# Stick-breaking attention of a decoder step: running sums over high and low parts, a new order of the pairs, absolute values shared between two engines

## The reference, cut to what matters

```python
z = jnp.einsum('bqhd,bkhd->bhqk', qb, kb).astype(jnp.float32) * scale + bias
log_1m = jnp.where(mask, jax.nn.log_sigmoid(-z), 0.0)
log_w = jax.nn.log_sigmoid(z) + lax.cumsum(log_1m, axis=3, reverse=True) - log_1m
w = jnp.where(mask, jnp.exp(log_w), 0.0)
outs.append(jnp.einsum('bhqk,bkhd->bqhd', w.astype(vb.dtype), vb))
```

## Time and profile before

| what | us |
|---|---|
| median of 3 runs (lowest, highest) | 2427.94 (2426.88, 2428.55) |
| the profiled execution | 2428.46 |
| its span | 2426.8 |
| PE busy | 2382.4 |
| DVE busy | 1241.0 |
| ACT busy | 994.5 |
| granted clock over the span | 0.998 |

### The profile page before, as it was taken

The page is one execution under the profiler, slowest core; times in us unless marked ns, Lnnn a source line. Parts: engine busy times, 40 slices in busy tenths (PEclk is TensorE's granted clock), DMA queues, the critical chain, the costliest instruction groups (busy, mean ns, idle before and its releaser), DMA issues.

```text
span 2426.8 us, 43808 instructions
## 1 busy us (share of the span) xinstructions
PE 2382.4 (98%) x18802; PEld 2183.8 (90%) x18802; DVE 1241.0 (51%) x1725; ACT 994.5 (41%) x1399; POOL 114.9 (5%) x232
## 2 busy tenths in 40 slices
PE   6999999999999999999999999999999999999998
PEld 5999999965699999999999999887777999999998
DVE  5533246755576333357523347755554758633245
ACT  5422235635456222346422245533223546522243
POOL 0000000122100000000000000012222100000000
PEclk9999999999999999999999999999999999999999
DMA  8555345785537653565754255544545456642254
GB/s 308 180 183 183 124 149 179 252 211 139 190 113 228 215 173 95 188 206 175 261 184 156 83 168 189 188 153 165 170 165 165 136 177 182 206 126 88 87 179 155
DMA packets 122660, 417.10 MB, mean 172 GB/s; under 512 B 23387, under 2 KB 27611, under 8 KB 122211
## 3 DMA queue, kind: packets, MB, share of 16 engines
q1 hardware_dynamic: 88962, 301.92, 39.1%
q10 hardware_dynamic: 18144, 62.03, 7.1%
q0 software_dynamic: 15360, 50.34, 6.3%
HBM read 390.84 MB, written 23.41 MB: 171 GB/s over the span
## 4 chain that ended last, share of the span: by engine, by line
PE 88%; DVE 5%; ACT 3%; DMA 2%; issue 1%; SPq 0%; ACTq 0%; POOL 0%; DVEq 0%; POOLq 0%
PE PS L2026 70%; PE PS L1425 3%; PE PS L1960 2%; DVE WL L2318 2%; PE PS L1990 2%; PE PS L1355 1%; ACT WH L2140 1%; DMA AFIRST<-in_w_ada 1%; PE PS L791 1%; PE PS L1309 1%; PE PS L1340 1%; PE PS L1350 1%; PE PS L753 1%; DMA RAW<-in_w_out 1%; PE PS L1321 1%
## 5 line engine op out<-in xcount | busy, mean ns | idle before, releaser
L2318 DVE TENSOR_TENSOR WL<-RAW,WH 128x1024 fp32r<-128x1024 f32 (+1 forms) x478 | 633.0, 1325 | 647.9 <-ACT WH L2140 647.2
L2026 PE MATMUL PS<-HH,WH 128*128 128x260 f32 x3432 | 796.6, 285 | 3.2 <-DVE QKVS L1119 1.8
L2026 PE MATMUL PS<-HH,WL 128*128 128x260 f32 x3432 | 786.5, 283 | 0.0
L2026 PE MATMUL PS<-HL,WH 128*128 128x260 f32 x3368 | 769.6, 283 | 0.0
L2140 ACT ACTIVATE WH<-RAW 128x1024 fp32r<-128x1024 f32 (+1 forms) x478 | 542.2, 1135 | 425.4 <-PE PS L2026 267.0
L2026 PEld LDWEIGHTS PS<-HH,WH 128*128 128x128 f32 x3432 | 569.9, 188 | 25.4 <-issue 16.8
L2026 PEld LDWEIGHTS PS<-HH,WL 128*128 128x128 f32 x3432 | 569.4, 188 | 0.0
L2026 PEld LDWEIGHTS PS<-HL,WH 128*128 128x128 f32 x3368 | 557.0, 188 | 0.6 <-issue 0.2
L2026 PE MATMUL PS<-GH,WH 128*128 128x260 f32 x1408 | 386.4, 285 | 0.9 <-DVE WL L2318 0.8
L2026 PE MATMUL PS<-GL,WH 128*128 128x260 f32 x1408 | 384.2, 283 | 0.0
L2026 PE MATMUL PS<-GH,WL 128*128 128x260 f32 x1408 | 383.5, 283 | 0.0
(11 more groups left out here) (340 smaller groups left out, 2317.5 us busy)
## 6 DMA issues: line engine op xcount, KB each, us to landing
RAW<-in_w_in SPq DMA_DIRECT2D x236, 512.0 KB, 3.7
RAW<-in_w_out SPq DMA_DIRECT2D x120, 704.0 KB, 4.0
AW<-in_w_ada ACTq DMA_DIRECT2D x114, 512.0 KB, 5.5
RAW<-in_w_odd SPq DMA_DIRECT2D x60, 512.0 KB, 3.7
RAW<-in_w_odout SPq DMA_DIRECT2D x30, 512.0 KB, 3.9
RAW<-in_w_even SPq DMA_DIRECT2D x28, 512.0 KB, 4.0
KV<-in_v_pages POOLq DMA_DIRECT2D x32, 256.0 KB, 4.8
SR<-in_ret_past POOLq DMA_DIRECT2D x32, 256.0 KB, 4.0
```

The lines of the kernel that those rows point to most:

```text
L2026: last = nc.tensor.matmul(ps[:, x, 0:HT], w[:, k * P:(k + 1) * P], src[k0 + k][:, x, :], start=(begin and t == 0), stop=(end and t == 2))
L2318: nc.vector.tensor_tensor(low_, RAW[:, from_:from_ + w], high_.bitcast(F32), ALU.subtract).then_inc(lo_done, 1)
```

## The change

It touches the mixer of the first layer alone.

- `sums` multiplies in fp32r: ACT copies the softplus rounded to fp32r into one of two places SPH (`high_part`), DVE takes the difference into SPL (`low_part`), which lies on SP itself, and each group runs both parts against fp32r copies TRIR and ONESR of the triangle and the ones: 20 fp32r matmuls for a head, where there were 10 in fp32.
- `log_weights` writes into SP, and ZS is free after it; SP has five places (`HOME_OF`).
- `sized` (absolute value by DVE) is for heads 0 to 3, ACT takes it for heads 4 to 7 (`decay`).
- The last units of evin have side work at four places. The scores of head 1, `sums_past` and, on ACT and DVE, the work on head 0 up to its high and low part stand in units 25 to 27.
- After evin, PE interleaves the scores of pair 1 with the sums of head 0; in the loop a turn runs sums, `values_past`, sums, all scores of pair t + 2, and the values of pair t.
- The outputs of k and of the pooling rows are issued before the loads of evout instead of between them, under a semaphore `pool_out` of their own, and the pooling rows are written 16 wide (`US[:]`); the host drops the first.

```diff
+HOME_OF = (0, 1, 2, 3, 0, 4, 2, 3)
+SP = [SQ5[n] for n in HOME_OF]
+SPL = [SL5[n] for n in HOME_OF]
+SPH = [at("SHA", [CAUSAL], sph_at, F32R)[:], at("SHB", [CAUSAL], sph_at + causal, F32R)[:]]
+TRIR = at("TRIR", [P], acc_at, F32R)
+ONESR = at("ONESR", [P], acc_at + size([P]), F32R)
...
-        if i == 3:
+        if i == 0:
             sp.wait_ge(ev_act, EV_FULL)
             sp.wait_ge(ev_dve, EV_FULL)
             for dst, src in ((k_t[:, 0:4 * SEQ], KP[:]), (k_t[:, 4 * SEQ:4 * SEQ + 32], QKVS[:, 4:8, :]),
-                             (pool_p, UP[:, :, SEQ + 1:SEQ + 16]), (pool_n, US[:, :, :, 1:16])):
-                sp.dma_start(dst, src).then_inc(out_done, 16)
+                             (pool_p, UP[:, :, SEQ + 1:SEQ + 16]), (pool_n, US[:])):
+                sp.dma_start(dst, src).then_inc(pool_out, 16)
+        if i == 3:
...
+        h, j = divmod(n, 3)
-            pe.wait_ge(z_dve, n)
+            pe.wait_ge(z_dve, 4 * h + j)
+        if n == 3:
+            pe.wait_ge(pool_low, 5)
...
+    POOLED_AT = {(23, 4): 0, (24, 2): 1, (24, 4): 2, (25, 2): 3}
+    SCORES_AT = {(25, 3): 0, (25, 4): 1, (26, 1): 2, (26, 2): 3, (26, 3): 4, (26, 4): 5}
+    def side(i, quarter):
+        if quarter == 4 and i in (22, 23, 24, 25):
             scores_past(i - 22)
+        if (i, quarter) == (26, 2):
             turn_past()
+        if (i, quarter) in POOLED_AT:
+            pooled(POOLED_AT[i, quarter])
+        if (i, quarter) in SCORES_AT:
+            first_scores(SCORES_AT[i, quarter])
+        if (i, quarter) == (27, 3):
+            sums_past()
...
-    def scores_of_one():
-        for j in range(4):
-            pe.wait_ge(vp_evac, 2) if j < 2 else pe.wait_ge(z_dve, 3 + j)
-            score(1, j, PS[0][:, j % 2, 0:LEN[j]]).then_inc(z_done, 1)
+            side(i, 4)
     def scores(t, j):
-        if t == PAIRS:
+        if t >= PAIRS:
             return
-        pe.wait_ge(z_dve, biased_to(t, j))
+        if t == 1 and j == 0:
+            pe.wait_ge(vp_evac, 2)
+        else:
+            pe.wait_ge(z_dve, 8 * t + 2 * j)
         for e in range(2):
             score(2 * t + e, j, PS[0][:, e, 0:LEN[j]]).then_inc(z_done, 1)
     def sums(h, i):
         if i == 0:
-            pe.wait_ge(sp_done, h + 1)
+            pe.wait_ge(spl_done, h + 1)
+        if h + i == 0:
+            pe.wait_ge(const_ok, 3)
         n = 4 * h + i
         pe.wait_ge(lw_done, n - 1) if n >= 2 else pe.wait_ge(vp_evac, 4)
-        last = nc.tensor.matmul(PS[1][:, i % 2, 0:LEN[i]], TRI[:], SP[h % 4][:, OFF[i]:OFF[i] + LEN[i]],
-                                start=True, stop=(i == 3))
-        for j in range(i + 1, 4):
-            last = nc.tensor.matmul(PS[1][:, i % 2, (j - i) * P:LEN[i]], ONES[:],
-                                    SP[h % 4][:, OFF[j]:OFF[j] + LEN[j]], start=False, stop=(j == 3))
+        for j in range(i, 4):
+            w = TRIR if j == i else ONESR
+            for x, part in enumerate((SPH[h % 2], SPL[h])):
+                last = nc.tensor.matmul(PS[1][:, i % 2, (j - i) * P:LEN[i]], w[:],
+                                        part[:, OFF[j]:OFF[j] + LEN[j]], start=(j == i and x == 0),
+                                        stop=(j == 3 and x == 1))
         last.then_inc(s_done, 1)
...
-    sums_past()
-    scores_of_one()
+    for j in range(4):
+        scores(1, j)
+        sums(0, j)
     ada_step("start", 0)
     for t in range(PAIRS):
-        scores(t + 1, 0)
-        sums(2 * t, 0)
-        scores(t + 1, 1)
         if t:
-            values(t - 1)
-        sums(2 * t, 1)
-        scores(t + 1, 2)
-        sums(2 * t, 2)
-        if t == 2:
-            gather(0)
-        scores(t + 1, 3)
-        sums(2 * t, 3)
-        if t < 3:
-            values_past(t)
+            for i in range(4):
+                sums(2 * t, i)
+        values_past(t)
         ada_step("head", 2 * t)
         for i in range(4):
             sums(2 * t + 1, i)
+        if t == 1:
+            gather(0)
+        for j in range(4):
+            scores(t + 2, j)
+        ada_step("head", 2 * t + 1)
         if t == 3:
-            values_past(3)
-        ada_step("head", 2 * t + 1)
-    gather(1)
-    values(3)
+            gather(1)
+        values(t)
...
     def decay(h):
-        act.wait_ge(z_masked, 4 * h + 4)
-        nc.scalar.activation(SP[h % 4], ZS[h % 4], ACT.Abs).then_inc(z_act, 1)
-        act.wait_ge(z_act, h + 1)
-        nc.scalar.activation(SP[h % 4], SP[h % 4], ACT.Exp, scale=-1.0).then_inc(e_done, 1)
+        if h > 3:
+            act.wait_ge(z_masked, block_of(h, 3))
+            act.wait_ge(o_done, h // 2 - 1)
+            nc.scalar.activation(SP[h], ZS[h], ACT.Abs).then_inc(z_abs, 1)
+        act.wait_ge(z_abs, h + 1)
+        nc.scalar.activation(SP[h], SP[h], ACT.Exp, scale=-1.0).then_inc(e_done, 1)
     def log(h):
         act.wait_ge(e_done, h + 1)
-        nc.scalar.activation(SP[h % 4], SP[h % 4], ACT.Ln, bias=ONES[:, 0:1]).then_inc(l_done, 1)
+        nc.scalar.activation(SP[h], SP[h], ACT.Ln, bias=ONES[:, 0:1]).then_inc(l_done, 1)
+    def high_part(h):
+        act.wait_ge(sp_done, h + 1)
+        if h == 0:
+            act.wait_ge(pool_out, 64)
+        after(act, s_done, 4 * (h - 2) + 4)
+        nc.scalar.activation(SPH[h % 2], SP[h], ACT.Copy).then_inc(sph_done, 1)
     def weights(h):
         act.wait_ge(lw_done, 4 * h + 4)
-        nc.scalar.activation(SP[h % 4], ZS[h % 4], ACT.Exp).then_inc(w_done, 1)
+        nc.scalar.activation(SP[h], SP[h], ACT.Exp).then_inc(w_done, 1)
...
     for t in range(PAIRS):
+        if t == 0:
+            weights(0)
+        if t < 3:
+            decay(2 * t + 2)
+            decay(2 * t + 3)
+            table(LOG_SET)
+            log(2 * t + 2)
+            log(2 * t + 3)
+            table(EXP_SET)
         if t:
             outputs(t - 1)
+            weights(2 * t)
+        weights(2 * t + 1)
         if t < 3:
-            decay_of_pair(t + 1)
-            table(LOG_SET)
-        if t < 3:
-            for h in (2 * t + 2, 2 * t + 3):
-                log(h)
-            table(EXP_SET)
-        for h in (2 * t, 2 * t + 1):
-            weights(h)
+            high_part(2 * t + 2)
+            high_part(2 * t + 3)
...
+    def sized(h):
+        dve.wait_ge(z_dve, block_of(h, 3))
+        dve.wait_ge(z_masked, block_of(h, 3))
+        nc.vector.scalar_tensor_tensor(SP[h], ZS[h], -1.0, ZS[h], ALU.mult, ALU.max).then_inc(z_abs, 1)
     def softplus(h):
+        if h >= HEADS:
+            return
         dve.wait_ge(l_done, h + 1)
-        dve.wait_ge(z_dve, 4 * h + 4 if h < 2 else sized_to(h // 2, h % 2))
-        nc.vector.scalar_tensor_tensor(SP[h % 4], ZS[h % 4], 0.0, SP[h % 4], ALU.max,
-                                       ALU.add).then_inc(sp_done, 1)
+        nc.vector.scalar_tensor_tensor(SP[h], ZS[h], 0.0, SP[h], ALU.max, ALU.add).then_inc(sp_done, 1)
+    def low_part(h):
+        dve.wait_ge(sph_done, h + 1)
+        nc.vector.tensor_tensor(SPL[h], SP[h], SPH[h % 2].bitcast(F32), ALU.subtract).then_inc(spl_done, 1)
     def log_weights(h, i):
         dve.wait_ge(s_done, 4 * h + i + 1)
-        z = ZS[h % 4][:, OFF[i]:OFF[i] + LEN[i]]
-        nc.vector.tensor_tensor(z, z, PS[1][:, i % 2, 0:LEN[i]], ALU.subtract).then_inc(lw_done, 1)
     def scored(t, j):
-        if t == PAIRS:
+        if t >= PAIRS:
             return
         if j == 0:
-            after(dve, w_done, 2 * t - 2)
-            if t == 1:
-                dve.wait_ge(out_done, 96)
+            after(dve, lw_done, 8 * (t - 1))
         for e in range(2):
             dve.wait_ge(z_done, 8 * t + 2 * j + e + 1)
             biased(2 * t + e, j, PS[0][:, e, 0:LEN[j]])
...
+            first_scored(0, 0)
+            first_scored(0, 1)
+            first_scored(0, 2)
+            first_scored(0, 3)
+            pooled_samples()
+            sized(0)
+            dve.wait_ge(pool_out, 64)
+            first_scored(1, 0)
+            first_scored(1, 1)
+            ada_evac("evin", i)
+        if i == 27:
+            first_scored(1, 2)
+            first_scored(1, 3)
+            ada_evac("evin", i)
+            sized(1)
+            low_part(0)
...
     dve.wait_ge(zn_pe, 2)
+    nc.vector.tensor_tensor(ZN[:, 0, :], ZN[:, 0, :], PS[2][:, 0, :], ALU.subtract).then_inc(zn_dve, 1)
     dve.wait_ge(unit_done, POS["evin"] + len(EV))
-    nc.vector.tensor_tensor(ZN[:, 0, :], ZN[:, 0, :], PS[2][:, 0, :], ALU.subtract).then_inc(zn_dve, 1)
-    scored_one()
+    scored(1, 0)
     nc.vector.tensor_copy(VSR[0:NS, :], PS[3][0:NS, 1, :]).then_inc(vs_ok, 1)
     dve.wait_ge(vs_ok, 1)
-    nc.vector.memset(PS[3][:, 1, :], 0.0).then_inc(pz_ok, 1)
+    nc.vector.memset(PS[3][:, 1, :], 0.0).then_inc(z_zero, 1)
+    log_weights(0, 0)
+    scored(1, 1)
+    log_weights(0, 1)
+    softplus(1)
+    scored(1, 2)
+    log_weights(0, 2)
+    scored(1, 3)
+    log_weights(0, 3)
+    sized(2)
+    low_part(1)
+    sized(3)
     for t in range(PAIRS):
-        if t == 2:
+        if t:
```

(35 more changed lines are left out.)

169 lines of the change are left out of this document (78 added, 91 removed).

## The result

The median after the change is 2440.97 us (2439.22 to 2443.39, five runs), before it 2428.55 (2426.88 to 2432.22): a ratio of 1.0049 with an interval of [1.0034, 1.0063], 0.5% slower. The prediction was 2431.3, in a range up to 2437. The change is slower, as forecast, but by 12.4 us and not by 3.4, so the prediction was wrong on size. The execution in the profile took 2440.05 us, with a span of 2438.4.

The account below looks back on a forecast made before the run. PE, busy for 98% of the span, was taken as the bound. Stretch terms 0.4 + 7.9 - 1.9 - 3.4 gave +3.0 us, raised to +3.4 for missed small delays: 2431.3 us, range 2426.5 to 2437.

Parts of the forecast that it names:

- The sums: On PE, a head's sums would take 3.1 us instead of 4.79, sparing 1.7 a head, 13.6 for eight heads.
- my lower bound: In the sums, an fp32r product of 128 columns takes at least 0.06 us; 0.10 was assumed.
- The scores in a row: Four score blocks in sequence between PE and DVE: steps of 2.6, 2.1, 1.6 and 0.43 us, 6.8 in all.
- The chain behind: After the last scores, DVE's biased scores, softplus and low part take 5.1 us; PE waits another 1.8 before the next sums.
- The earlier output of k costs nothing: it goes while PE is in evin, whose loads are far ahead: During evin, issuing k's output earlier was claimed to add 0 us.
- no more than 3 us: Bound on the early k output: without cover it would delay a gather by its own transfer, at most this.
- The clock: Rival: thin PE work between scores and sums drops the clock, 6.3 us more each of two times, 2444 us; chance 0.04.
- PE is there after 13.3 and waits 1.1: At the last values_past, pages land after 14.4 us; PE arrives after 13.3 and waits 1.1.
- The new order as such: In the attention, the reordered work and split sums together were laid out as +3.0 us, raised to +3.4.
- the four stretches: PE from scores_past(1) to first values_past, sums of head 2, sums of head 6, first output product: 62.7, 20.2, 40.7, 18.2 us.
- The layout: Step-by-step schedule of PE's work and waits through the attention, giving +3.0 us; 2428 to 2435 by itself, weight 0.66.
- the three named: PE's waits before the change: 1.05 us for the samples' softplus, 0.99 for head 1's, 0.34 at pair 3.

Follow-up runs that it names:

- e3: The change with unread filler matmuls in the waits between the blocks of scores of pairs 2 and 3: 2443.87 us, ratio 1.0059.
- e2: The kernel before with only k's two outputs issued early, ahead of evout's first load: 2439.07 us, ratio 1.0040.
- e1: The change with k's two outputs back at their old place, the pooling rows still early: 2437.52 us, ratio 1.0034.
- e7: e1 with the sums in fp32 again, without high and low parts, in the new order: 2441.43 us, ratio 1.0047.
- b1_split: The kernel before in its own order, with split fp32r sums for all heads and pooling rows in whole lines: 2447.71 us, ratio 1.0073.
- b3_odd: The kernel before in its own order, with the sums of heads 3, 5 and 7 alone split: 2428.66 us, ratio 0.9996.

## Why the prediction was wrong, and where it was right

**The sums: right in total, by the luck of two misses that cancel.** 3.31 us a head; I had 3.1, and 3.4 with waits for PS[1]. The short products cost less than I took:

```profile
604.51 0.22 PE L811 MATMUL PS<-SHA,ONESR 128*128 128x128 f32 x1
604.57 0.27 PE L811 MATMUL PS<-SCL,ONESR 128*128 128x128 f32 x1
```

0.06 us, my lower bound. At the measured spacings the 20 products make 2.3 us, and 0.24 us for each of the four groups is left, where I had 0.1. FP8 and Floating Point Precision (TensorE Precision Notes), of the Trainium skill, led to an estimate of 2.4 us for a head; the products alone come to that, but no head does, the waits for PS[1] included in its time.

**The scores in a row: right. The chain behind: about right.** Steps of 2.69, 2.15 and 1.67 us for 2.6, 2.1 and 1.6. Waits for a low part of 1.0 us at heads 4 and 6, none at head 2, where I had 1.8 to 2.8; the lower clock had stretched the values ahead of them, and e3 brought the waits back, 1.81 and 2.85 at heads 2 and 4.

**"The earlier output of k costs nothing: it goes while PE is in evin, whose loads are far ahead": wrong**, the step that failed worst. I asked whether evin's weights had slack, and not whose loads share the time: `scores_past(2)` needs eight page loads of 256 KB, asked for from 510 us on, and k goes at 512.5. They took 7.6 us to land (median), not 3.6. PE waited 4.16 us and then ran 3 us longer at the lower clock. My bound, "no more than 3 us", had the transfer and left out what follows a wait. The pooling rows, moved to the same place, have their share: with only k early the wait is 0.84 us (e2), with only the pooling rows early 0.70 (e1). I had only asked what their whole lines free, and not what their new place costs. DMA: Bandwidth & Descriptors (Issuing engines are not separate DMA queues), of the Trainium skill, says that transfers of all issuing engines run on the same 16 DMA engines and interleave; the trace agrees: POOL's page loads and SP's output are on different queues, and the loads landed 1.7 to 4.0 us later with the outputs beside them.

**The clock, given a chance of 0.04: happened, at four places.** I named the place between scores and sums and its price, 6.3 us each time. The price was wrong: the modulation step and the values took 2.5 us longer (5.77 us from 597.58 to 603.35, for 1.0 + 2.3), and most of that replaced a wait: e3 got back 0.9 and 0.7 us. Ahead of the first `values_past` the lower clock took 3.0 in the change; in e1_k_late 0.9, at the modulation step at 575.3 us. TensorE: Matmul & The Clock Gate (HAM oscillation), of the Trainium skill, warned of such a relapse for groups of matmuls between waits. The trace agrees with it in kind; the 2444 that I gave for this rival was nearer to the 2441 than my forecast, but by luck: no stretch bears out its 6.3 us.

**"PE is there after 13.3 and waits 1.1": half right.** The wait for the last value pages was 2.31 us, and behind it `values_past` ran at a clock of 0.58, 4.02 us for its first ten products which took 2.32 in the call at 606.67. These 1.2 and 1.7 us are what is missing at the end, 2.7.

**The new order as such: mis-sized.** I had +3.0 us for order and split together. e1_k_late, the change without the early k, is +8.4, and e7, without the split as well, +11.3. In e1's profile the four stretches are 1.9, 1.7, 0.4 and 2.6 us longer than laid out. The layout had no term for the clock, which explains 0.9 us in the first stretch, 1.6 in the last (3.87 us for the first ten products of `values_past`, for 2.32) and, by e3, some 0.9 in the second. Waits for pages explain another 0.70 in the first and 1.1 in the last. The rest, 1.4 us, stays open. The prediction also read the old order as better than it is: the longest wait there for biased scores is not among the three named,

```profile
613.96 0.92 PE L685 MATMUL PS<-QP,KP 64*128 64x384 f32 x4 [1.49 <-DVE ZD L1056]
```

so the exchange of scores between PE and DVE cost something before too.

## What to carry to other kernels

A shorter product on the bounding engine is worth its time only where the passes that feed it have slack: list for each consumer when its input is ready and when it is wanted, and change only those with a gap. Before moving a large output, look at every load in flight in the stretch it moves to, on any queue, and price a late load as its wait plus, where the wait is long, the work behind it at half the clock (the waits of 0.70 and 0.84 us left the clock at 1.00, that of 4.16 did not). When a wait is filled or a clock restored, look for the next wait before counting the gain.

## What was not expected of the hardware

- Outputs of 1 MB (k) and 256 KB (pooling rows) beside page loads of 256 KB doubled their landing, 3.6 to 7.6 us; k alone made it 5.3 and the pooling rows alone 6.0. POOL's own issues went from 1.15 us apart to 2.1 (514.60, 516.71, 518.85).
- Writing 4096 pieces of 60 bytes (packets under 512 B fall from 23387 to 19290 without them) kept the queues busy until 555 us (DMA share 1.48 at 65 GB/s); with whole lines issued at the same place (b1_split) the share in that stretch is 0.00. Page loads issued behind the pieces needed 16.5 us (median, kernel before) and 19.9 us (e2). That PE waited for nothing there before was luck: b3_odd, with the same transfers, waited 2.0 us.
- The granted clock fell to 0.50 not only behind one long wait (4.16 us) but also behind short ones with little work between: at pair 2 during the third wait, behind waits of 1.57 and 1.23 us with blocks of scores of 0.7 to 1.1 us (590 to 596 us), and at pair 3 already at the end of the second (619.8 us).
